# Twenty-one projection pairs of each layer as seven products instead of eight

## The reference

```
h = rms_norm(x, norm_mix[l])
z = einsum('btd,dn->btn', h, w_in[l])      # 1024 -> 88 tiles of 128, plus 24 small columns
a_q, a_k, a_v, b_q, b_k, b_v, b_g, b_lr, c_qkv, c_z, c_b, c_a, gates = split(z)
x += W_o( sum_b sigmoid(gate_b) * P_b(mixer_b) )   # A windowed attention, B gated linear attention, C gated DeltaNet
x += FFN(rms_norm(x, norm_ffn[l]))                 # layer 0 dense SwiGLU, layer 1 top-2 of 8 experts
```

## Time and profile before

| | |
|---|---|
| three runs, median | 1810.05 us (1804.7 to 1813.07) |
| span of the profiled execution | 1802.1 us |
| TensorE busy | 1748.8 us, 97% |
| VectorE, ScalarE, GpSimd busy | 743.5, 364.3, 154.3 us |
| projection matmuls (L940) | 2816 instructions, 654.3 us busy |
| idle of TensorE just before a projection matmul | 0.0 us |

### The profile page before, as it was taken

One profiled execution on the slowest core, in us unless ns is written; L12 is line 12 of the kernel. 1 busy time (PEld: TensorE's weight loads), 2 busy tenths in 40 slices (PEclk: granted clock), 3 DMA queues, 4 the chain that ended last, 5 costly groups with the idle time before them and its releaser, 6 DMA issues.

```text
span 1802.1 us, 30183 instructions
## 1 busy us (share of the span) xinstructions
PE 1748.8 (97%) x12542; PEld 1282.9 (71%) x12542; DVE 743.5 (41%) x1548; ACT 364.3 (20%) x760; POOL 154.3 (9%) x259
## 2 busy tenths in 40 slices
PE   9999999999999999999999998999989999999997
PEld 7889888787768999978898887877663343333423
DVE  3444542434535765534544414355342332233222
ACT  2241333433101000012313333331011110100001
POOL 3000000403200111000100002032000000000000
PEclk9999999999999999999999999999999999999999
DMA  9833599999999997899535899899958999999994
GB/s 296 285 120 100 187 324 316 359 310 367 388 347 392 365 321 286 288 348 371 194 107 207 308 325 346 312 350 384 333 211 327 393 377 414 402 398 394 371 415 177
DMA packets 265853, 563.96 MB, mean 313 GB/s; under 512 B 14654, under 2 KB 163362, under 8 KB 265441
## 3 DMA queue, kind: packets, MB, share of 16 engines
q1 hardware_dynamic: 246384, 500.15, 76.8%
q0 software_dynamic: 18544, 58.58, 9.2%
q10 hardware_dynamic: 784, 3.26, 0.5%
...
## 4 chain that ended last, share of the span: by engine, by line
PE 85%; SPq 7%; DMA 4%; DVE 2%; issue 1%; ACT 1%; DVEq 0%; POOL 0%; ACTq 0%; POOLq 0%
PE PS L940 34%; PE PS L1598 8%; PE PS L1374 8%; SPq L811 7%; PE PS L1350 5%; PE PS L1382 4%; PE PS L859 3%; PE PS L986 3%; PE PS L1576 3%; PE PS L1364 2%; PE PS L979 2%; PE PS L1636 2%; PE PS L1321 1%; PE PS L1537 1%; DMA mem<-bias_tables 1%
## 5 line engine op out<-in xcount | busy, mean ns | idle before, releaser
L940 PE MATMUL PS<-h,mem 128*128 128x264 f32 x2816 | 654.3, 389 | 0.0
L940 PEld LDWEIGHTS PS<-h,mem 128*128 128x128 f32 x2816 | 527.8, 191 | 106.7 <-issue 21.3
L1806 ACT COPY z<-PS 128x264 f32<-128x264 f32 (+5 forms) x293 | 119.5, 430 | 737.6 <-PE PS L940 527.6
L1598 PE MATMUL PS<-mem,z 128*32 128x512 f32 (+1 forms) x1536 | 146.1, 523 | 3.8 <-DMA mem<-in_moe_w_up 3.8
L2893 DVE COPY small<-mem 128x1024 f32 x56 | 38.8, 693 | 175.6 <-PE PS L1576 117.8
L1598 PEld LDWEIGHTS PS<-mem,z 128*32 128x32 f32 x1536 | 47.4, 110 | 77.8 <-issue 61.2
L1576 PE MATMUL PS<-small,z 128*32 128x256 f32 (+2 forms) x624 | 86.9, 396 | 1.3 <-DVE z L2893 1.3
L1350 PE MATMUL PS<-z,mem 128*128 128x264 f32 x384 | 87.3, 388 | 0.0
L1576 PE MATMUL PS<-z 128*32 128x256 f32 (+2 forms) x624 | 87.0, 396 | 0.0
L1350 PEld LDWEIGHTS PS<-z,mem 128*128 128x128 f32 x384 | 72.3, 190 | 13.8 <-issue 1.7
L1374 PE MATMUL PS<-z,mem 128*128 128x132 f32 x624 | 78.3, 278 | 0.0
...
## 6 DMA issues: line engine op xcount, KB each, us to landing
out_win_s<-in_cache_win_kv SPq DMA_DIRECT2D x128, 1023.5 KB, 11.9
...
```

The source lines that it names most:

```text
L940: last = mm(bank(l, "p", j)[:, 0:T], w[:, k, P * (j % 2):P * (j % 2) + P], h[:, k, :], start=(k == 0), stop=(k == KT - 1))
L1598: last = mm(m_bank("c", "gu", g, b, w, r)[BLK * j:BLK * j + BLK, 0:n], hs[:, k, P * r + BLK * j:P * r + BLK * j + BLK], v3(slot_ap(set_slo ...
L1806: return nc.scalar.copy(out, in_)
```

## The change

Twenty-one of the 44 pairs of each layer (q = 8 to 11, 15 to 19, 23 to 31, 33, 35, 37) are computed with seven products of four half-width matmuls, 28 instead of 16 full-width ones. Their two steps `proj` each become `fold_x`, `fold_y` and `fold_x2`, `fold_y2`; with `around` one of each two stands where half a tile stood. A new step `fold_w` on GpSimd makes three sums of weight quarters and one difference in place in the chunk; it is put behind the first product step of the pair before, or behind the tile before. `fold_h` on VectorE makes four sums of `h` once in a layer. They lie in the place of x, which SyncE writes to memory before (`x_kept`) and reads back after the last such pair. The sums' buffers are free stretches of z and of the arena. VectorE reads the results of x, y and y2 from the banks, ScalarE that of x2; x and x2 both use bank 0, y and y2 both bank 1. The number of chunk slots stays five.

```diff
@@ -51,6 +51,9 @@
 
 S_TAB, S_KEY, S_SELF, S_TOT = 0, NG * 512, NG * 512 + NG * P, NG * 512 + NG * P + NS
 
+HALF = T // 2
+UNSETTLED = ("proj", "fold_x", "fold_y", "fold_x2", "fold_y2", "fold_w")
+FOLD = (8, 9, 10, 11, 15, 16, 17, 18, 19, *range(23, 32), 33, 35, 37)
 WARM = 12
 CH_PROJ, CH_WB, CH_WO = Z_N // 2, 6, 4
 MERGE = (1, 2, 0)
@@ -80,8 +83,14 @@
     s = [("params",), ("xnorm", 0)] + [("tables",)] * (l == 0) + [("small",)]
     proj = iter(range(Z_N))
 
+    def tile(j):
+        q = j // 2
+        if q not in FOLD:
+            return [("proj", j)]
+        return [("fold_x2", q), ("fold_y2", q)] if j % 2 else [("fold_x", q), ("fold_y", q)]
+
     def p(n=1):
-        return [("proj", next(proj)) for _ in range(n)]
+        return [step for _ in range(n) for step in tile(next(proj))]
 
     s += p() + [("small_turn",)] + p(2) + [("conv_v", 0)] + p() + [("gate_c",)] + p() + [("conv_v", 1)]
     for j in range(2, 6):
@@ -90,7 +99,8 @@
     s += [("norm_sq", 0)] + p() + [("norm_sum", 0), ("norm_sq", 1)] + p() + [("norm_sum", 1)] + p()
     def around(*step):
         j = next(proj)
-        return [step, ("proj_half", j), (step[0] + "2", *step[1:]), ("proj", j)]
+        first, rest = tile(j) if j // 2 in FOLD else (("proj_half", j), ("proj", j))
+        return [step, first, (step[0] + "2", *step[1:]), rest]
 
     for i in range(TT):
         s += [("gdn_dec", i)] + p() + around("gdn_a", i)
@@ -118,6 +128,10 @@
     s += [("mg", 2, 0), ("mg", 2, 1), ("mg", 2, 2), ("as_v", 1), ("as_o",), ("mg", 2, 3)]
     s += [("mg", 0, q) for q in range(4)] + [("bar", 1), ("wo",)]
     assert next(proj, None) is None
+    s.insert(s.index(("proj", 3)) + 1, ("fold_h",))
+    for q in FOLD:
+        before = ("fold_x", q - 1) if q - 1 in FOLD else ("proj", 2 * q - 2)
+        s.insert(s.index(before) + 1, ("fold_w", q))
     return s
 
...
@@ -610,7 +631,7 @@
         for l in range(DEPTH):
             n0 = CH0[l]
             for q in range(CH_PROJ):
-                place(n0 + q, q % RING, (l, "p", 2 * q + 1))
+                place(n0 + q, q % RING, (l, "fold_y2", q) if q in FOLD else (l, "p", 2 * q + 1))
             for q in range(CH_WB):
                 place(n0 + CH_PROJ + q, (CH_PROJ + q) % RING, (l, "mb", MERGE[q // 2], KT - 1))
             for q in range(CH_WO):
...
@@ -748,6 +770,37 @@
         def bc(ap, axis, shape):
             return ap.unsqueeze(axis).to_broadcast(shape)
 
+        zflat = z.rearrange("p a b -> p (a b)")
+        S_LA, S_SIG, S_G0, S_G1, S_K0, S_K1 = range(6)
+        FOLD_SETS = [[arena[:, 8800 + 512 * n:9312 + 512 * n] for n in range(3)],
...
+        def fold_set(q):
+
+            return (S_G0 if q >= 30 else S_LA if q >= Z_K // 2 else S_K0) + q % 2
+
+        def fold_before(q):
+
+            same = [r for r in FOLD if r < q and fold_set(r) == fold_set(q)]
+            return same[-1] if same else None
+
+        def fold_sums(q):
+
+            return [v3(b, 4) for b in FOLD_SETS[fold_set(q)]]
+
+        def fold_quarters(l, q):
+
+            w = v3(chunk(CH0[l] + q), KT)
+            return w[:, 0:4, 0:P], w[:, 4:8, 0:P], w[:, 0:4, P:2 * P], w[:, 4:8, P:2 * P]
+
+        def fold_out(q):
+
+            return z[:, 2 * q:2 * q + 2, :].rearrange("p a b -> p (a b)")
+
...
@@ -837,7 +904,14 @@
                     if l == 0 and n == CH_MIX + RING:
                         sp.wait_ge(sems["bar_v"], V("bar_v", 0, 1))
                         sp.wait_ge(sems["bar_a"], V("bar_a", 0, 1))
+                    if n == RING:
+                        sp.wait_ge(sems["h_ready"], V("h_ready", l, KT - 1))
+                        sp.dma_start(x_kept[l], x_flat).then_inc(x_in, 16)
                     load(CH0[l] + n, source(l, n))
+                    if n == FOLD[-1] + RING:
+                        wait_full(sp, l, "fold_y2", FOLD[-1])
+                        sp.wait_ge(x_in, 64 + 32 * l)
+                        sp.dma_start(x_flat, x_kept[l]).then_inc(x_in, 16)
                     shift_some(l, n)
             assert not pieces
             for name in ("bar_v", "bar_a", "bar_p"):
@@ -948,6 +1022,40 @@
 
             def proj(l, j):
                 proj_ks(l, j, range(4, KT) if (l, j) in halved else range(KT))
+
+            def four(out, left, right, opens=False):
+
+                for k in range(4):
+                    last = mm(out, left[:, k, :], right[:, k, :], start=(opens and k == 0), stop=(k == 3), skip_group_check=True)
+                return last
+
+            def fold_x(l, q):
+                wait_chunk(pe, CH0[l] + q)
+                open_bank(pe, l, "fold_x", q)
+                x_ = bank(l, "fold_x", q)
+                four(x_[:, 0:HALF], fold_quarters(l, q)[0], h[:, 0:4, 0:HALF], True)
+                pe.wait_ge(hd_ready, h_sum(l, 3))
+                pe.wait_ge(fw_even, even_sum(l, q, 1))
+                four(x_[:, HALF:T], fold_sums(q)[1], fold_t[:, 1]).then_inc(full(l, "fold_x", q), 1)
+
+            def fold_y(l, q):
+                pe.wait_ge(fw_odd, odd_sum(l, q))
+                open_bank(pe, l, "fold_y", q)
+                y_ = bank(l, "fold_y", q)
+                four(y_[:, 0:HALF], fold_sums(q)[0], fold_t[:, 0], True)
+                four(y_[:, HALF:T], fold_quarters(l, q)[2], fold_t[:, 2]).then_inc(full(l, "fold_y", q), 1)
+
+            def fold_x2(l, q):
+                open_bank(pe, l, "fold_x2", q)
+                four(bank(l, "fold_x2", q)[:, 0:HALF], fold_quarters(l, q)[1], h[:, 4:8, 0:HALF]).then_inc(
+                    full(l, "fold_x2", q), 1)
+
+            def fold_y2(l, q):
+                open_bank(pe, l, "fold_y2", q)
+                y_ = bank(l, "fold_y2", q)
+                four(y_[:, HALF:T], fold_quarters(l, q)[3], fold_t[:, 3])
+                pe.wait_ge(fw_even, even_sum(l, q, 2))
+                four(y_[:, 0:HALF], fold_sums(q)[2], h[:, 4:8, HALF:T]).then_inc(full(l, "fold_y2", q), 1)
 
             def conv_s(l):
                 pe.wait_ge(convt_in, 16 * (l + 1))
...
@@ -1841,6 +1949,10 @@
                     act.wait_ge(stored["glas"], 32 * (l + 1))
                 wait_full(act, l, "p", j)
                 copy(z[:, j, :], bank(l, "p", j)[:, 0:T]).then_inc(free(l, "p", j), 1)
+
+            def fold_x2(l, q):
+                wait_full(act, l, "fold_x2", q)
+                copy(fold_out(q)[:, 0:HALF], bank(l, "fold_x2", q)[:, 0:HALF]).then_inc(free(l, "fold_x2", q), 1)
 
             def small_turn(l):
                 act.wait_ge(sems["xa_ready"], V("xa_ready", l))
...
@@ -2227,6 +2339,36 @@
                 dve.wait_ge(sems["g_exp"], V("g_exp", l))
                 link(stt(xa, xa, 0.0, gl, MAX, ADD))
                 stt(gl, xa, -1.0, bc(ealog, 1, [P, 3, 4]), MUL, MUL).then_inc(sems["g_ready"], 1)
+
+            def fold_h(l):
+                dve.wait_ge(x_in, 64 + 32 * l)
+                h11, h12, h21, h22 = h[:, 0:4, 0:HALF], h[:, 0:4, HALF:T], h[:, 4:8, 0:HALF], h[:, 4:8, HALF:T]
+                tt(fold_t[:, 0], h12, h11, SUB)
+                tt(fold_t[:, 2], h22, h12, SUB).then_inc(hd_ready, 1)
+                dve.wait_ge(hd_ready, h_sum(l, 1))
+                tt(fold_t[:, 1], h22, fold_t[:, 0], SUB).then_inc(hd_ready, 1)
+                dve.wait_ge(hd_ready, h_sum(l, 2))
+                tt(fold_t[:, 3], h21, fold_t[:, 1], SUB).then_inc(hd_ready, 1)
+
+            def fold_x(l, q):
+                if q != FOLD[0]:
+                    wait_read(dve, l, "fold_y2", FOLD[FOLD.index(q) - 1])
+                wait_full(dve, l, "fold_x", q)
+                nc.vector.tensor_reduce(fold_ve[:, 0, :], bank(l, "fold_x", q)[:, 0:T].rearrange("p (w t) -> p t w", w=2),
+                                        AX.X, ADD).then_inc(free(l, "fold_x", q), 1)
+
+            def fold_y(l, q):
+                wait_full(dve, l, "fold_y", q)
+                nc.vector.tensor_reduce(fold_ve[:, 1, :], bank(l, "fold_y", q)[:, 0:T].rearrange("p (w t) -> p t w", w=2),
+                                        AX.X, ADD).then_inc(free(l, "fold_y", q), 1)
+                wait_read(dve, l, "fold_x", q)
+                wait_read(dve, l, "fold_y", q)
+                tt(fold_out(q)[:, 3 * HALF:4 * HALF], fold_ve[:, 0, :], fold_ve[:, 1, :], ADD)
+
+            def fold_y2(l, q):
+                wait_full(dve, l, "fold_y2", q)
+                tt(v3(fold_out(q)[:, HALF:3 * HALF], 2), v3(bank(l, "fold_y2", q)[:, 0:T], 2),
+                   bc(fold_ve[:, 0, :], 1, [P, 2, HALF]), ADD).then_inc(free(l, "fold_y2", q), 1)
 
             def conv_v(l, n):
                 wait_z(dve, l, 2 * n, 2 * n + 2)
...
@@ -2650,6 +2792,7 @@
                     last.then_inc(sems["acc_ready"], 1)
 
             def wo(l):
+                dve.wait_ge(x_in, 80 + 32 * l)
                 for d in range(KT):
                     wait_full(dve, l, "wo", d)
                     tt(x[:, d, :], x[:, d, :], bank(l, "wo", d)[:, 0:T], ADD).then_inc(free(l, "wo", d), 1)
...
@@ -3048,6 +3192,28 @@
                 for w in range(2):
```

(23 more changed lines are left out.)

73 lines of the change are left out of this document (47 added, 26 removed).

## The result

The changed kernel takes 1830.6 us (median of 4 runs, 1824.5 to 1833.5), the kernel before 1807.4 beside it (4 runs, 1802.9 to 1813.1): ratio 1.0133, 95% interval 1.0111 to 1.0155. That is 23 us slower, where 5.4 were forecast. It lies in the range of 1799 to 1832, but outside the forecast's own 1806 to 1825; the forecast was "within 0.5%", and the size is wrong by four times. The profiled execution of after has a span of 1831.4 us against 1802.1, 29.3 more. It was the slowest of its four, with a mean granted clock of 0.978, that of before had 0.993; so the profiles overstate the loss by about 6 us.

The account below looks back on a forecast made before the run. TensorE, busy 97% of the span, was taken to bound the kernel. Costs of 18.1 us a layer, 36.2 us, against 30.8 gained made it 5.4 us slower: 1815.5 us, own range 1806 to 1825, overall range 1799 to 1832.

Parts of the forecast that it names:

- GpSimd's order and the stop: At pair 15, GpSimd's sums stand behind the inverses' transfers, so TensorE stops 10.3 us in each layer.
- the bank of pair 8: End of the convolution: x2 waits for VectorE to empty bank 0, 2.5 us a layer, bounds 0.3 and 3.9.
- decay and ScalarE's copy: Pair 11 and tile 24: x2's copy stands behind ScalarE's eight exponentials and frees the bank late, 1.0 us a layer.
- The gain: Products in 21 pairs and two layers: fewer TensorE instructions save 0.73 us a pair, 30.8 us in all.
- After such a stop TensorE runs slowly for a while: Behind the stop at pair 15: lower clock costs 1.8 us once in each layer, 3.6 us, bounds 0 and 7.
- The levels: DeltaNet levels: reduces and GpSimd's sums come on top of a tight chain, 0.5 us a layer, bounds 0 and 2.6.
- Contention: VectorE and GpSimd hold each other up, within the terms for pair 8 (2.5), norms (1.3) and levels (0.5 us a layer).
- norms: Seven pairs a layer after a norm: VectorE's reduce frees the bank exactly at the limit, 1.3 us a layer, bounds 0 and 6.
- What costs nothing: Writing x out and back and VectorE's four sums over it are covered by VectorE's idle time in the convolution: 0 us.
- The second: Rival: VectorE and GpSimd take turns, tight-path instructions each losing a 1.21 us sum; 21.8 us slower, 1832 us; chance 0.23.
- The first: Rival: GpSimd reaches pair 15's sums in time, no stop or slow clock; 18.8 us faster, 1791 us; chance 0.17.
- The third: Rival: GpSimd's sums delay the third score step's tables, about 2 us a layer lost; 1820 us; chance 0.10.

Follow-up runs that it names:

- experiment 4: Kernel before, without products, with one TensorE wait added: long at tile 30, 1825.2 us; short at tile 17, 1814.9 us.
- experiment 2: Changed kernel with GpSimd's sums of pair 15 ahead of the inverses' transfers and sums over 8 columns instead of 512: 1793.9 us.
- experiment 6: Changed kernel with pairs plain: 15, 1811.9 us; 15 to 19, 1806.3; 8, 15, 31 and VectorE's sums later, 1795.8; this last also without 16 to 19, 1796.6.
- experiments 3: Changed kernel with all projection pairs plain, GpSimd making 20 pairs' sums for nobody: whole sums 1817.6 us, over 8 columns 1800.5 us.
- small sums alone: Changed kernel with all projection pairs plain, GpSimd's unused sums of 20 pairs over 8 columns instead of 512: 1800.5 us.

## Why the prediction was wrong

- **Right**: GpSimd's order and the stop (10.3 forecast, 10.36 and 10.42), the bank of pair 8 (2.5; 2.18 and 2.06), decay and ScalarE's copy (1.0; 1.33). The gain was taken a little low, 0.73 us a pair for 0.81 at the undisturbed pace, 34.2 us; the text had named 34.4. Net of the clock, TensorE's busy time fell by only 28 us.
- **The step that failed** is "After such a stop TensorE runs slowly for a while ... I add that 1.8 us once in each layer". Behind the stop it was about 2.5 us a layer, near enough. The error was "once": 35 us of full-speed time are not had in the runs of after and 17 in those of before, and stops alone bring 2 to 3 (experiment 4). Less the 5 us that lie inside the stops, the term is about 13 us where I put 3.6, and 19.7 in the profiled execution.
- **The levels were under-sized, and not for contention.** I put 0.5 us a layer on them, and it was 2.6 with what is behind them. Only 0.6 of that goes with GpSimd's load; 2.0 is there without it (experiment 2) and goes with pairs 16 to 19 (experiment 6). For 1.4 of it the rows show VectorE's reduces ahead of what TensorE waits for; I had named them and not sized them.
- **Contention** as a wait was not under-sized in sum: 8.6 us for pair 8, norms and levels, and about 7 in after. But I left out that VectorE's scalings wait too, each for itself. In after the stop at pair 15 covers that; without the stop it is 1.8 us a layer (experiments 3 and 6). And the sums alone cost 17 us, of which such waits are 6.
- **"What costs nothing"** failed for the parking: I named the cover (VectorE idles before each pair of tiles) and overlooked the gate's small instructions behind `fold_h`, for which ScalarE's queue waits. 2.1 us in the profile; in the time it can't be seen.
- **The rivals.** The second said 1832, and the time was 1830.6. That is luck: the two engines do take turns, but its terms for it (3.9, 6 and 2.6 us a layer) were 2.1, 0.8 and 0.6, and the clock, which it left at 3.6, filled the difference. The first fell. The third did not show: the wait before the scores is 9.2 us in after against 8.2 (1.4 longer in layer 1, 0.4 shorter in layer 0), but VectorE waits there for the first tables, which are not issued behind sums; at the third score step TensorE doesn't wait.
- **Open**: what lowers the clock in kernels with whole sums. Those without them lie at 14 to 22 us in the table's last column, those with them at 21 to 35. The sums are not all of it: products with small sums have 22, small sums alone 14. Many short waits of TensorE are one candidate; that several engines work at once is another. No run here tells them apart. Nor do I know why the first blocks of the experts run slowly in some executions.
